# Down products of an expert step run one step later, turned results in two buffers, and a split moved at the second mixer's seam

## The chip, the cores and the metric

The kernel runs on one NeuronCore of one Trainium2 chip. The metric is the device time of one execution in microseconds (us), lower is better. Five engines work beside each other: PE (TensorE, matrix products), DVE (VectorE), ACT (ScalarE), POOL (GpSimd) and SP (SyncE, which here only issues weight loads). They wait for each other through semaphores.

## The reference

A trunk of two residual layers on 256 tokens of width 1024, all float32. Each layer has a mixer (attention and a short gated convolution) and a channel mixer. The channel mixer of the first layer is a dense SwiGLU, that of the second sends each token to 2 of 8 experts:

```python
def swiglu(h, w_gu, w_down):
    gu = h @ w_gu
    g, u = jnp.split(gu, 2, axis=-1)
    return (jax.nn.silu(g) * u) @ w_down

def moe_swiglu(h, router_w, w_gu, w_down):
...
    for e in range(N_EXPERTS):
        out = out + cw[:, e:e + 1] * swiglu(xf, w_gu[e], w_down[e])
```

An expert has 1024 x 7168 gate and up weights and 3584 x 1024 down weights, so that 44 MB are read for each.

## The kernel before, in words

**Halves.** All weights come in pieces of 128 x 2048 floats, 1 MB each, which the kernel calls halves. SP loads a half into one of six slots of `w_raw`. ACT rounds it to a high part (`split_hi`, line 397 or 394), DVE forms the low part as the difference (`split_lo`, line 406 or 403), and PE then multiplies the high and low parts. The parts of a half in the expert section also rotate over six slots (`moe_hi`, `moe_lo`: three of `w_hi`/`w_lo`, then `e_k`/`e_uy`, `hT`/`e_v`, `e_q`/`e_bias`). So the load of half n waits until the low part of half n-6 stands (`lo_ready`), and the split of half n waits until PE has used half n-6 (`half_used`).

**Blocks.** The expert section is eight blocks here, one for each expert, of 42 halves each. Blocks 0, 2, 4 and 6 are wide: 128 tokens, `product` with three products of 512 columns (lines 410 to 412) for each of four pieces, so 12 products to a half. Blocks 1, 3, 5 and 7 are narrow: at most 64 tokens, whose high and low parts lie side by side in one operand, so `both_parts` has two products (lines 1808, 1809) and a half has 8.

**Steps.** A block has seven steps m of 512 hidden columns. A step has four gate and up halves (gate into bank 0, up into bank 1, `up`) and two down halves (`down`, into banks 4 and 5, which gather the whole block). I number the halves of a block 0 to 41 in the order in which PE uses them. Between up and down the hidden values must be turned: in a wide block ACT takes silu of bank 0 (`silu`, line 930), DVE multiplies by bank 1 (`gated`, line 1391), PE transposes into bank 2 (`turn`, line 1814), ACT and DVE make its high and low part (`turn_hi` line 934, `turn_lo` line 1395, tiles `ffT_hi` and `ffT_lo`, which are parts of `cT_hi` and `cT_lo`). In a narrow block ACT copies both banks (`take_gate` line 939, `take_up` line 943), PE turns them and adds the two token halves in one product with the matrix `fold` (`fold_turn`, line 1823), ACT takes silu (`fold_silu`, 947), DVE multiplies (`fold_prod`, 1399), ACT rounds (`fold_hi`, 951), DVE subtracts (`fold_lo`, 1403).

**Order of PE before.** In a step: gate, up, down of the step before, then the turn of this step. A block ends with: down of step 5 (halves 38, 39), turn of step 6, `gather` of the next block's tokens (line 1787, 32 small products, copied to SBUF by `gathered` on ACT line 915/918 and DVE line 1370/1373; its fourth group waits for ACT's first copy), down of step 6 (halves 40, 41). The next block then scales and adds what stands in banks 4 and 5: `take_y` (line 925 on ACT, 1378 on DVE), `scatter` (line 1851) and `add_scattered` (1385).

**Who sets the order.** Every engine's order is written out by hand in its own block; nothing is scheduled. Each engine works strictly in its order.

**Routing.** `route` on DVE ranks the experts; a chain of small POOL instructions then makes the seat tables and ends with `route_ready` (line 708). DVE's first `next_pick` (line 1354) waits for it, in block 0, between the splits of halves 14 and 15. The first `gather` waits for `fold_ready`, the last of `route`'s results (line 1342).

**The second mixer's seam.** Between the dense part and the mixer of layer 2 stands `norm(2)`: DVE adds the sums (line 1121), ACT squares (737), DVE finds the root in a chain of tiny instructions (1096 to 1102) and scales (1109), PE transposes (1580), ACT and DVE split (743, 1126). The second half of that mixer's weights is split by ACT inside the norm and, for its low part, by POOL (`norm_split`).

## Time and profile before

| | us |
|---|---|
| median of 3 runs | 1782.83 (1782.44 to 1782.89) |
| profiled execution | 1784.56 |
| its span, first to last instruction | 1782.7 |
| PE busy | 1669.4 (94%) |
| DVE busy | 1317.7 (74%) |
| ACT busy | 1118.9 (63%) |
| POOL busy | 208.4 (12%) |

The weight loads' queue takes 71.1% of 16 DMA engines' span; 485 MB are read. The expert section runs from about 810 us to 1767 us. Busy shares are averages over stages with different limits, so the rows further below go stage by stage. A row of the timeline gives start, duration, engine, line, tiles and count, and in brackets the idle time of the engine ahead of it and who ended it. The granted clock is given as a share of TensorE's full 2.4 GHz; 0.5 is 1.2 GHz.

### The profile page before, as it was taken

The numbers are of one execution on the slowest core, as the hardware profiler recorded it, in microseconds if no ns is written. First come the engines' busy times: TensorE is split into PE (matmuls) and PEld (weight loads), VectorE is DVE, ScalarE is ACT, GpSimd is POOL, SyncE is SP. The second block draws the span as 40 slices with busy tenths as digits, with TensorE's granted clock in tenths as the row PEclk, the third lists the DMA queues.
The fourth block names the chain that finished last, engine by engine and source line by source line (L and its number), as shares of the span: only waits on it lengthen the run. The fifth ranks groups of instructions, "written<-read, shape, count | busy, mean of one in ns | idle before, by whom it ended". The sixth has DMA issues, their size and how long they took to land.

```text
span 1782.7 us, 22550 instructions
## 1 busy us (share of the span) xinstructions
PE 1669.4 (94%) x7827; PEld 1371.3 (77%) x7827; DVE 1317.7 (74%) x1156; ACT 1118.9 (63%) x1120; POOL 208.4 (12%) x434
## 2 busy tenths in 40 slices
PE   6999999999979999978999989999899999899996
PEld 4888887888768888866787778887778877788784
DVE  4456756544454676566788989889988799898896
ACT  4456643434335567335677877778867688677794
POOL 1034331000010344228200000000000000000000
PEclk8999999999989999977999999999999999999998
DMA  6644554555535445535798999989999989999893
GB/s 267 251 165 166 177 182 151 195 184 190 186 112 180 166 160 177 192 128 207 295 382 331 407 401 348 378 326 397 422 347 365 367 333 423 377 356 376 331 417 144
DMA packets 71783, 488.37 MB, mean 274 GB/s; under 512 B 8667, under 2 KB 11948, under 8 KB 13228
## 3 DMA queue, kind: packets, MB, share of 16 engines
q1 hardware_dynamic: 69052, 483.89, 71.1%
q10 hardware_dynamic: 2672, 3.70, 0.6%
q8 instruction: 36, 0.59, 0.1%
q14 instruction: 23, 0.19, 0.0%
HBM read 484.94 MB, written 2.62 MB: 274 GB/s over the span
## 4 chain that ended last, share of the span: by engine, by line
PE 68%; DVE 14%; issue 7%; DMA 4%; ACT 3%; POOL 3%; DVEq 0%; SPq 0%; ACTq 0%; POOLq 0%
PE bank L410 21%; PE bank L412 20%; PE bank L411 20%; DVE w_lo L406 5%; DMA w_raw<-expert_slabs 4%; DVE e_v L403 3%; DVE e_uy L406 2%; POOL wgtT L699 1%; ACT hT L394 1%; PE bank L1808 1%; DVE e_bias L406 1%; PE bank L1809 1%; PE bank L1649 1%; ACT w_hi L397 1%; PE bank L1814 1%
## 5 line engine op out<-in xcount | busy, mean ns | idle before, releaser
L406 DVE TENSOR_TENSOR w_lo<-w_raw,w_hi 128x2048 fp32r<-128x2048 f32 x285 | 648.8, 2290 | 278.1 <-ACT w_hi L397 277.0
L397 ACT ACTIVATE w_hi<-w_raw 128x2048 fp32r<-128x2048 f32 x289 | 552.0, 1915 | 357.5 <-PE bank L412 351.9
L410 PE MATMUL bank<-w_hi,hT 128*128 128x512 f32 x1072 | 428.1, 399 | 9.7 <-DVE hT L1126 8.9
L412 PE MATMUL bank<-w_hi,hT 128*128 128x512 f32 x1072 | 421.7, 393 | 0.0
L411 PE MATMUL bank<-w_lo,hT 128*128 128x512 f32 x1072 | 421.4, 393 | 0.0
L410 PEld LDWEIGHTS bank<-w_hi,hT 128*128 128x128 f32 x1072 | 204.0, 190 | 54.2 <-DVE hT L1126 10.8
L412 PEld LDWEIGHTS bank<-w_hi,hT 128*128 128x128 f32 x1072 | 203.7, 190 | 43.8
L411 PEld LDWEIGHTS bank<-w_lo,hT 128*128 128x128 f32 x1072 | 204.2, 190 | 41.0
L406 DVE TENSOR_TENSOR e_bias<-w_raw,e_q 128x2048 fp32r<-128x2048 f32 x55 | 125.7, 2286 | 44.5 <-ACT e_q L397 44.5
L397 ACT ACTIVATE e_q<-w_raw 128x2048 fp32r<-128x2048 f32 x55 | 105.6, 1920 | 55.6 <-PE bank L412 36.9
L406 DVE TENSOR_TENSOR e_uy<-w_raw,e_k 128x2048 fp32r<-128x2048 f32 x56 | 129.9, 2320 | 7.4 <-ACT e_k L397 7.1
L403 DVE TENSOR_TENSOR e_v<-w_raw,hT 128x2048 fp32r<-128x2048 f32 x55 | 125.9, 2289 | 10.8 <-ACT hT L394 10.8
L397 ACT ACTIVATE e_k<-w_raw 128x2048 fp32r<-128x2048 f32 x56 | 107.4, 1917 | 30.8 <-PE bank L412 19.7
L1808 PE MATMUL bank<-w_hi,hT 128*128 128x512 f32 x320 | 125.0, 391 | 0.0
L1809 PE MATMUL bank<-w_lo,hT 128*128 128x512 f32 x320 | 124.6, 389 | 0.0
L394 ACT ACTIVATE hT<-w_raw 128x2048 fp32r<-128x2048 f32 x55 | 105.5, 1918 | 24.0 <-PE bank L412 18.0
L1808 PEld LDWEIGHTS bank<-w_hi,hT 128*128 128x128 f32 x320 | 60.1, 188 | 12.7
L1809 PEld LDWEIGHTS bank<-w_lo,hT 128*128 128x128 f32 x320 | 60.1, 188 | 12.5
L410 PE MATMUL bank<-w_hi,cT_hi 128*128 128x512 f32 x168 | 65.9, 392 | 1.5 <-DVE cT_lo L1270 1.5
L412 PE MATMUL bank<-w_hi,cT_lo 128*128 128x512 f32 x168 | 65.5, 390 | 0.0
L411 PE MATMUL bank<-w_lo,cT_hi 128*128 128x512 f32 x168 | 65.4, 389 | 0.0
L1823 PEld LDWEIGHTS bank<-wgt,part 128*128 128x128 f32 x448 | 54.0, 191 | 4.1 <-ACT part L943 1.6
(328 smaller groups left out, 2473.4 us busy)
## 6 DMA issues: line engine op xcount, KB each, us to landing
w_raw<-expert_slabs SPq DMA_DIRECT2D x334, 1024.0 KB, 7.0
w_raw<-mix_slabs SPq DMA_DIRECT2D x88, 1024.0 KB, 4.8
w_raw<-dense_slabs SPq DMA_DIRECT2D x33, 1024.0 KB, 4.8
bias_lines<-bias ACTq DMA_DIRECT2D x2, 768.0 KB, 4.4
X<-in_x SPq DMA_DIRECT2D x2, 512.0 KB, 4.1
bias<-bias_lines SPq DMA_DIRECT2D x1, 1024.0 KB, 7.2
yT<-in_ffn_norm_g ACTq DMA_DIRECT2D x2, 512.0 KB, 5.6
v_buf<-expert_slabs SPq DMA_DIRECT2D x1, 1024.0 KB, 4.8
```

Source lines behind the costliest of these rows:

```text
L394: act.activation(hi_slot(n), in_pair(raw_of(n, early)), ACT.Copy).then_inc(hi_ready, 1)
L397: act.activation(hi_slot(n), raw_of(n, early), ACT.Copy).then_inc(hi_ready, 1)
L403: eng.tensor_tensor(in_pair(lo_slot(n)), in_pair(raw_of(n, early)), hi_slot(n), ALU.subtract).then_inc(lo_ready, 1)
L406: eng.tensor_tensor(lo_slot(n), raw_of(n, early), hi_slot(n), ALU.subtract).then_inc(lo_ready, 1)
L410: pe.matmul(dst, hi, whi, start=first, stop=False, skip_group_check=True)
L411: pe.matmul(dst, hi, wlo, start=False, stop=False, skip_group_check=True)
L412: return pe.matmul(dst, lo, whi, start=False, stop=last, skip_group_check=True)
L699: chain(pool.tensor_tensor(terms[:, :, c, :], src[:, r:r + 2, :], col_no[:, c:c + 1, :].to_broadcast([P, 2, 2 * EXPERTS]), ALU.mult))
L1649: ins = pe.transpose(bank[4 + t][:, P * c:P * c + P], tok_c(rows)[:, t, P * c:P * c + P], ident[:, :])
L1808: pe.matmul(dst, x, whi, start=first, stop=False, skip_group_check=True)
L1809: return pe.matmul(dst, x, wlo, start=False, stop=last, skip_group_check=True)
L1823: ins = pe.matmul(bank[2][:, at:at + NARROW], raw[:, P * j:P * j + P], fold[:, :], start=True, stop=True, skip_group_check=True)
```

## The change

In the expert section the down products of step m-1 move behind gate and up of step m+1: PE's step is now gate(m), turn(m-1), up(m), down(m-2). The block ends with turn(6), gather, down(5), down(6). Since two turned results now live at a time, `ffT_hi`/`ffT_lo` get a second buffer (`zero_r` and a free part of `cT_lo`), picked by the step's parity. SP's loads, ACT's and DVE's lists follow this order; the splits of the next block's halves 42 and 43 (0 and 1 of the next) now stand ahead of the copies of the gathered tokens, that of 44 behind them, and the last two gate/up halves of step 0 in `begin`. New waits: PE's `turn` and `fold_turn` wait for `e_lo` (bank 2 read), each step for `e_silu` (bank 0 read), `silu` and `gated` for a stated `half_used`, `take_gate` for `e_turn`. PE's wait for `fold_ready` moves from ahead of the first gather to behind block 0. At `norm(2)` the split of the mixer's second half stands ahead of the norm on ACT and on DVE; POOL's instruction goes.

```diff
                 def load_step(m, cyc):
                     for i in range(4):
-                        load_half(sp, MOE0 + 4 + i, gate_up(i, m), cyc)
+                        load_half(sp, MOE0 + 8 + i, gate_up(i, m), cyc)
                     for i in range(2):
-                        load_half(sp, MOE0 + 8 + i, down_rows(i, m - 1), cyc)
+                        load_half(sp, MOE0 + 12 + i, down_rows(i, m - 2), cyc)
...
             for layer in range(DEPTH):
-                if layer:
-                    norm_split(2)
-                else:
+                if layer == 0:
                     pool.wait_ge(gsub_ready, 1)
...
             def norm(q):
+                if q == 2:
+                    split_lo(dve, NORM_AT[q] + 1)
                 if q:
                     add_sums(q, 0)
...
             def norm(q):
+                if q == 2:
+                    split_hi(act, NORM_AT[q] + 1)
                 norm_sums(q, 0)
...
                 def narrow_block(b, i2, closing=False):
...
+                    with act.Fori(0, 2) as it:
+                        for j in range(2):
+                            cm = c + 2 * it + j
+                            m = 2 * it + 2 + j
+                            fold_silu(b, m - 1)
+                            take_gate(b, m, MOE0 + 10 + RAW * cm)
+                            split_hi(act, MOE0 + 16, cm)
+                            fold_hi(i2, m - 1, (j + 1) % 2)
+                            take_up(MOE0 + 12 + RAW * cm)
+                            for i in range(17, 22):
+                                split_hi(act, MOE0 + i, cm)
+                    fold_silu(b, MSTEPS - 2)
+                    take_gate(b, MSTEPS - 1, MOE0 + 34 + RAW * c)
+                    split_hi(act, MOE0 + 40, c)
+                    fold_hi(i2, MSTEPS - 2, 1)
+                    take_up(MOE0 + 36 + RAW * c)
+                    split_hi(act, MOE0 + 41, c)
+                    if not closing:
+                        split_hi(act, MOE0 + 42, c)
+                        split_hi(act, MOE0 + 43, c)
+                    fold_silu(b, MSTEPS - 1)
+                    if not closing:
                         gathered(b + 1, 0)
-                    fold_hi(i2, MSTEPS - 1)
+                    fold_hi(i2, MSTEPS - 1, 0)
                     if not closing:
                         gathered(b + 1, 2)
+                        split_hi(act, MOE0 + 44, c)
...
                 def turn(b, m):
                     pe.wait_ge(e_rows, MSTEPS * b + m + 2)
+                    pe.wait_ge(e_lo, MSTEPS * b + m + 1)
...
-                    down(MOE0 + 8, c, b, 0, two, first=True)
-                    turned(b, 1)
-                    with pe.Fori(2, MSTEPS) as m:
-                        cm = c + m - 1
-                        up(MOE0 + 4, cm, 0, two)
-                        up(MOE0 + 6, cm, 1, two)
-                        down(MOE0 + 8, cm, b, m - 1, two)
-                        turned(b, m)
+
+                    def step(n, m, cyc, par, first=False):
+                        pe.wait_ge(e_silu, MSTEPS * b + m)
+                        up(n, cyc, 0, two)
+                        turned(b, m - 1)
+                        up(n + 2, cyc, 1, two)
+                        down(n + 4, cyc, b, m - 2, par, two, first)
+
+                    step(MOE0 + 8, 2, c, 0, first=True)
+                    with pe.Fori(0, 2) as it:
+                        for j in range(2):
+                            step(MOE0 + 14 + 6 * j, 2 * it + 3 + j, c + 2 * it, (j + 1) % 2)
+                    turned(b, MSTEPS - 1)
                     if not closing:
                         pe.wait_ge(spread_ready, 2 * b + 2)
                         if not opening:
                             pe.wait_ge(x_add, 4 * b + 4)
                         gather(b + 1)
-                    down(MOE0 + BLOCK_HALVES - 2, c, b, MSTEPS - 1, two)
-
-                pe.wait_ge(fold_ready, 1)
+                    down(MOE0 + BLOCK_HALVES - 4, c, b, MSTEPS - 2, 1, two)
+                    down(MOE0 + BLOCK_HALVES - 2, c, b, MSTEPS - 1, 0, two)
+
                 gather(0)
                 block(0, opening=True)
...
                 last = pe.value_load(ctl_i[0:1, 0:1], min_val=EXPERTS - 1, max_val=EXPERTS - 1 + SLOTS)
+                pe.wait_ge(fold_ready, 1)
```

What the lists of the engines look like at three places, first before and then after the change (line numbers of the changed kernel are a few higher; ISA, REGISTER_ALU and branch rows only set up what follows).

DVE at the second mixer's seam: the dense part's last rows, then the norm. Before:

```order
L1265 TENSOR_TENSOR rows<-bank,part 128x256
L1276 REGISTER_ALU
L1276 COMPARE_AND_BRANCH
L1270 TENSOR_TENSOR cT_lo<-bank,cT_hi 128x512
L1121 TENSOR_TENSOR X<-X,bank 128x512 x2
L1096 TENSOR_SCALAR nw<-ssq 128x1
```

and after:

```order
L1273 TENSOR_TENSOR rows<-bank,part 128x256
L1284 REGISTER_ALU
L1284 COMPARE_AND_BRANCH
L1278 TENSOR_TENSOR cT_lo<-bank,cT_hi 128x512
L407 TENSOR_TENSOR w_lo<-w_raw,w_hi 128x2048
L1127 TENSOR_TENSOR X<-X,bank 128x512 x2
L1102 TENSOR_SCALAR nw<-ssq 128x1
```

One split, which stood in POOL's list, now stands ahead of DVE's two additions.

PE at the end of a narrow block, from the turn of step 6 (`wgt,part`) over the gather (`aT_hi`, `aT_lo`) to the first down product. Before, with down of step 5 ahead of these rows:

```order
L1823 MATMUL bank<-wgt,part 128x64 x8
L1894 REGISTER_ALU
L1894 COMPARE_AND_BRANCH
L1903 REGISTER_ALU
L1780 ISA
L1787 MATMUL bank<-cT_hi,aT_hi 128x128 x16
L1787 MATMUL bank<-cT_hi,aT_lo 128x128 x8
L1783 REGISTER_ALU
L1787 MATMUL bank<-cT_hi,aT_lo 128x128 x8
L1828 REGISTER_ALU
L1830 REGISTER_ALU
L1808 MATMUL bank<-e_q,cT_hi 128x512
```

and after, with down of step 4 ahead of them:

```order
L1830 REGISTER_ALU
L1831 REGISTER_ALU
L1836 MATMUL bank<-wgt,part 128x64 x8
L1921 REGISTER_ALU
L1791 ISA
L1798 MATMUL bank<-cT_hi,aT_hi 128x128 x16
L1798 MATMUL bank<-cT_hi,aT_lo 128x128 x8
L1794 REGISTER_ALU
L1798 MATMUL bank<-cT_hi,aT_lo 128x128 x8
L1843 REGISTER_ALU
L1819 MATMUL bank<-e_k,zero_r 128x512
```

The first product behind the gather was that of half 40 (`e_q`) with the result turned just before; now it is that of half 38 (`e_k`) with the result of step 5 in the second buffer.

DVE at the same place, from `fold_prod` of step 6 (`rows<-bank,rows`). Before:

```order
L1399 TENSOR_TENSOR rows<-bank,rows 128x256
L1492 REGISTER_ALU
L1492 COMPARE_AND_BRANCH
L1367 REGISTER_ALU
L1373 CAST hT<-bank 128x512
L1402 REGISTER_ALU
L1403 TENSOR_TENSOR cT_hi<-rows,cT_hi 128x4x64
L1367 REGISTER_ALU
L1373 CAST hT<-bank 128x512
L401 ISA
L406 TENSOR_TENSOR e_bias<-w_raw,e_q 128x2048
```

and after:

```order
L407 TENSOR_TENSOR w_lo<-w_raw,w_hi 128x2048
L1407 REGISTER_ALU
L1408 TENSOR_TENSOR rows<-bank,rows 128x256
L1375 REGISTER_ALU
L1381 CAST hT<-bank 128x512
L1411 REGISTER_ALU
L1412 TENSOR_TENSOR cT_hi<-rows,cT_hi 128x4x64
L1375 REGISTER_ALU
L1381 CAST hT<-bank 128x512
L402 REGISTER_ALU
L407 TENSOR_TENSOR e_uy<-w_raw,e_k 128x2048
L402 ISA
```

Behind the two copies of gathered tokens (`hT<-bank`) came the split of half 46, counted on from this block, and four splits of the next block were done; now two are done, and 44 follows.

## Rows read from the trace of the kernel before

**Rows 1.** Page, section 2: GB/s moved in each of 40 slices of the span

```profile
GB/s 267 251 165 166 177 182 151 195 184 190 186 112 180 166 160 177 192 128 207 295 382 331 407 401 348 378 326 397 422 347 365 367 333 423 377 356 376 331 417 144
```

**Rows 2.** Timeline, PE: turns of two successive steps of wide block 0

```profile
890.97 0.60 PE L1814 MATMUL bank<-ident,rows 128*128 128x128 f32 x4
...
907.77 0.60 PE L1814 MATMUL bank<-ident,rows 128*128 128x128 f32 x4
```

**Rows 3.** Stretch of narrow block 1: length, then busy us (instructions) by engine, clock, DMA

```profile
946.50:1058.10 111.60, 101.81 (x502) 83.88 (x502) 104.20 (x72) 91.41 (x76) 0.00 (x0) 0.97 0.95 384
```

**Rows 4.** Timeline, DVE: from one fold_lo to the next in narrow block 1

```profile
1002.04 0.41 DVE L1403 TENSOR_TENSOR cT_hi<-rows,cT_hi 128x256 fp32r<-128x256 f32 x1
1002.37 6.70 DVE L406 TENSOR_TENSOR w_lo<-w_raw,w_hi 128x2048 fp32r<-128x2048 f32 x3
...
1015.93 0.41 DVE L1403 TENSOR_TENSOR cT_hi<-rows,cT_hi 128x256 fp32r<-128x256 f32 x1
```

**Rows 5.** Timeline, ACT: split of half 39 of narrow block 1

```profile
1037.62 1.92 ACT L394 ACTIVATE hT<-w_raw 128x2048 fp32r<-128x2048 f32 x1 [0.57 <-DMA w_raw<-expert_slabs]
```

**Rows 6.** Timeline, four engines: the second mixer's seam

```profile
493.20 1.28 DVE L1121 TENSOR_TENSOR X<-X,bank 128x512 f32<-128x512 f32 x2 [3.17 <-PE bank L412]
...
494.57 1.06 ACT L737 ACTIVATE part<-X 128x1024 f32<-128x1024 f32 x1 [5.26 <-DVE X L1121]
...
497.68 4.50 DVE L1101 TENSOR_TENSOR nw<-nw 128x1 f32<-128x1 f32 x1
...
497.67 4.49 POOL L406 TENSOR_TENSOR w_lo<-w_raw,w_hi 128x2048 fp32r<-128x2048 f32 x1 [191.14 <-ACT w_hi L397]
...
503.74 1.97 PE L1580 MATMUL bank<-ident,q_buf 128*128 128x128 f32 x8 [7.86 <-DVE q_buf L1109]
```

**Rows 7.** Timeline, DVE and PE: block 0 while routing ends

```profile
861.93 0.17 DVE L1354 COPY seat<-seats 128x5 f32<-128x5 f32 x1 [9.53 <-POOL ctl_i L708]
...
863.31 2.28 DVE L403 TENSOR_TENSOR e_v<-w_raw,hT 128x2048 fp32r<-128x2048 f32 x1
...
866.33 0.79 PE L410 MATMUL bank<-e_k,cT_hi 128*128 128x512 f32 x1 [4.18 <-DVE cT_lo L1395]
...
874.18 0.60 PE L1814 MATMUL bank<-ident,rows 128*128 128x128 f32 x4
```

**Rows 8.** Timeline, PE and ACT: ends of wide blocks 0 and 6

```profile
941.37 0.60 PE L1814 MATMUL bank<-ident,rows 128*128 128x128 f32 x4
...
946.46 0.79 PE L410 MATMUL bank<-e_q,cT_hi 128*128 128x512 f32 x1 [0.97 <-DVE cT_lo L1395]
...
953.84 1.27 ACT L925 ACTIVATE cT_hi<-bank,gate 128x512 fp32r<-128x512 f32 x2 [0.92 <-PE bank L412]
...
1653.30 0.60 PE L1814 MATMUL bank<-ident,rows 128*128 128x128 f32 x4
...
1664.32 1.27 ACT L925 ACTIVATE cT_hi<-bank,gate 128x512 fp32r<-128x512 f32 x2 [0.89 <-PE bank L412]
```

**Rows 9.** Timeline, DVE and PE: end of narrow block 1, start of wide block 2

```profile
1039.57 2.29 DVE L403 TENSOR_TENSOR e_v<-w_raw,hT 128x2048 fp32r<-128x2048 f32 x1 [0.20 <-ACT hT L394]
...
1055.23 1.76 PE L1787 MATMUL bank<-cT_hi,aT_lo 128*128 128x128 f32 x8 [2.02 <-ACT hT L918]
1058.14 0.79 PE L1808 MATMUL bank<-e_q,cT_hi 128*128 128x512 f32 x1 [1.14 <-DVE cT_hi L1403]
1075.71 0.49 PE L410 MATMUL bank<-e_q,hT 128*128 128x512 f32 x1 [0.84 <-ACT part L930]
```

**Rows 10.** Stretch at the same seam (columns as in Rows 3)

```profile
1055.40:1062.30 6.90, 5.76 (x18) 4.70 (x19) 3.21 (x5) 1.25 (x3) 0.00 (x0) 0.51 1.02 423
```

**Rows 11.** Page, section 5: weight loads of all 28 narrow turns, 16 each

```profile
L1823 PEld LDWEIGHTS bank<-wgt,part 128*128 128x128 f32 x448 | 54.0, 191 | 4.1 <-ACT part L943 1.6
```

**Rows 12.** Timeline, DVE and ACT: end of the last narrow block

```profile
1750.02 2.29 DVE L403 TENSOR_TENSOR e_v<-w_raw,hT 128x2048 fp32r<-128x2048 f32 x1 [0.21 <-ACT hT L394]
...
1766.90 1.26 ACT L925 ACTIVATE cT_hi<-bank,gate 128x512 fp32r<-128x512 f32 x2 [4.62 <-PE bank L1809]
```

304 lines of the change are left out of this document (150 added, 154 removed).

## The prediction, made before the changed kernel ran

> **What bounds the kernel now.** I read the page first, then the busy times of stretches, then the timelines of each kind of seam. The expert section is more than half of the span, and its two kinds of block have two different bounds.
>
> A wide step takes 16.80 us from turn to turn [rows 2]. Its 72 products and four transposes follow each other without a gap: with 0.36 us for the transposes and 0.13 us to get going, a half takes 2.72 us and 24 products 5.44 us. PE is the bound. A narrow step takes 13.89 us [rows 4]: six low parts at about 2.2 us and two fold operations at 0.33 us of pitch leave DVE without idle time. DVE is the bound there, 104.2 us busy of 111.6 in block 1 [rows 3], and PE, with 8 products or 1.82 us for a half and 1.7 us for a fold turn (54.0 us over 28 turns is 1.9, less the tail that overlaps the next product) [rows 11], would need 12.6. In the last two steps of a narrow block ACT waits for the load itself [rows 5]; at about 420 GB/s [rows 1] a half of 1.049 MB takes 2.5 us.
>
> So a step in mid-block has nothing to give: where PE is the bound it doesn't wait, and where it waits it isn't the bound. What can be won lies at the seams.
>
> **Steady steps: 0.** Both kinds keep their instructions, bytes and slots. In a wide step the new wait for `e_rows` at turn(m-1) is fed by a multiplication that can start after up(m-1); at least 10 us of down and gate products hide it. In a narrow step `take_up` now follows `fold_hi` of the step before, which follows DVE's split of the half that PE needs just ahead of that turn; copy and PE's half end together, about 1.4 and 1.8 us after that split. Behind that wait in PE's list stands up(m), but it has to wait for DVE's next split anyway. If the cover were gone, each of some 24 narrow steps would pay what is missing.
>
> **The second mixer's seam: 3.9 us less.** DVE's tiny L1101 takes 4.50 us instead of 0.16, together with POOL's split of 4.49 [rows 6]. POOL's goes, so 4.34 come back. DVE's own split (2.3 us) lies where DVE idles 3.17 us, and ACT's where ACT idles 5.26 [rows 6]: ACT is free at 489.3, rounds until 491.2, DVE subtracts until 493.7, 0.5 us after it was wanted at 493.2. 4.34 - 0.5 = 3.9. PE's idle 7.86 us shrinks to about 4; if the low clock behind it stays until the same time, 2 us are left; if it ends early, 6.
>
> The same row meets a rule of the Trainium skill, SBUF — State Buffer, section "Who interferes with whom": DVE with two SBUF inputs and GpSimd exclude each other for a whole instruction. By that rule the stall is POOL's doing and goes with it; were it chance, the term would be -0.5. The trace agrees with the rule, 4.50 beside 4.49.
>
> **The opening of block 0: 3.7 us less.** The first gather no longer waits for the fold matrix, and starts 5 to 6 us sooner; but the end of routing, at 861.93 on DVE [rows 7], hangs on POOL's chain and stays. DVE is held there, between the splits of 14 and 15, before as after; half 15 is ready at 863.31 + 2.2 = 865.5. Before, PE also wanted the turned result of step 1 for halves 14 and 15, started them at 866.33 after 4.18 idle and reached the next turn at 874.18: 7.85 us for 5.44 us of products, so 2.4 went to the low clock. Now halves 14 and 15 are gate(3): 14 is done before the stall, only 15 is left at 865.5. PE idles longer, about 7 us, so I charge the low clock again: 15 takes some 5 us, to 870.5. 874.2 - 870.5 = 3.7; without the low clock it waits for `gated` until 869.0, and 5.2 are won; with a longer one 2.
>
> **Wide to narrow, four seams: 7.6 us less.** Before, from the last turn (941.37) PE gathers, waits 0.97 us for the turned low part, and multiplies halves 40 and 41 [rows 8]. Now it gathers and multiplies 38 to 41, while ACT and DVE make the parts. For DVE, the bound of what follows, the time counts from "half 37 used" to ACT's `take_y`. Before: halves 38 and 39 (5.44) and 941.37 to 953.84 (12.47), 17.9. Now turn and gather 4.1, four halves 10.9, 0.3 to start: 15.3. That wins 2.6. The last such seam, without the low clock, had 1653.30 to 1664.32, 11.02: 16.5, so 1.15. Of the four seams two are of either kind: 2 x 2.6 + 2 x 1.15 = 7.6 (5 to 9). From `take_y` on, DVE has the same list and the loads stand as far ahead.
>
> **Narrow to wide, three seams: 13.2 us less.** Count from the end of DVE's split of half 39, 1039.57 + 2.2 = 1041.8 [rows 9]. Before, PE needs down(5), turn(6), the gather with 2.02 us idle for ACT's copy, 1.14 us idle for `fold_lo`, down(6) at a clock of 0.51 [rows 10], the next block's first four halves, and after 0.84 us for silu it starts the fifth at 1075.7: 33.9 us; the three seams lie within 0.8 us. Now: `fold_prod`, `fold_hi`, `take_up`, at 1.4; turn(6) to 3.1; three gather groups to 5.9. ACT's first copy now stands behind the splits of 41, 42 and 43 and `fold_silu`. The landings pace these at 2.5 us each, so it ends at about 8.2. The fourth group ends at 9.1, down(5) at 12.8, down(6) at 16.4, four wide halves at 27.3. PE is the bound from here, so 6.6 us are won, 6.4 over the three, with no low clock. But PE runs right behind DVE at the end of a narrow block and now sits idle before turn(6): half 37 is used 1.8 us after its split, turn(6) may start 6.3 us after it, 4.4 us idle. Before this idle was 1.5. Like the 4.18 us of rows 7 it should bring the low clock; part of it lies beside the wait for the copy. I charge 2.0 (0 to 3.5): 4.4 x 3 = 13.2 (9 to 19).
>
> **The last block: 2.0 us less.** From split 39 (1752.2) to `take_y` (1766.90) 14.7 us [rows 12]. Now turn(6) at 3.1, then down(5), down(6): 11.0 with 0.3 to start 11.2, 3.5 less; 1.5 for the low clock.
>
> **Sum.** 3.9 + 3.7 + 7.6 + 13.2 + 2.0 = 30.4. The profiled execution took 1784.56 with a span of 1782.70; it would come to 1754.2, the span to 1752.3. The median of 1782.83 lies 1.7 below that execution, so 1752.4 for the new median.
>
> **Rivals.**
> *The clock eats the seams.* The long idle before turn(6) brings a low clock that lasts over gather and down(5), down(6). 3.5 to 4 us more of such products at half speed than I charge would leave 1 us at each of the three seams, 0 in the last block, 2.5 in block 0, 2.5 at the mixer's: 2.5 + 2.5 + 7.6 + 3 = 15.6, 1767. For: 0.51 in rows 10 after smaller gaps.
> *No low clock at all.* 3.9 + 5.2 + 7.6 + 19.2 + 3.5 = 39.4, 1743.4. For: two wide-to-narrow seams had 1 us of idle and none.
> *Loads take it back.* What DVE wins at the start of a narrow block it waits for at its end, since loads were already late there: 30.4 - 7.6 = 22.8, 1760. Against: the load's lead is rebuilt in each wide block, where a half takes 2.72 us and a load 2.5.
> *Slower.* In narrow steps PE no longer has the down products as a backlog; it waits for each half from DVE, 0.4 us six times. If these gaps bring the low clock often, PE becomes the bound: 12.6 us of work take 12.6/(1 - f/2) when a share f of the time is at 0.5. That passes 13.9 at f = 0.19, and the 30 us are gone, over 24 steps, at 15.2 us a step, f = 0.34. At f = 0.45 a step takes 16.3: 24 x 2.4 - 30 = +27, 1810. Against: gaps of 0.9 us once a step left the clock of block 1 at 0.97 [rows 3], and a slow stretch closes the gaps that caused it.
> A page bears on this rival: the Trainium skill, TensorE: Matmul & The Clock Gate, section "HAM oscillation — how this bites in real kernels", tells of a kernel whose products wait for every slice of weights and begin each at the low clock. No row here shows that for gaps as short as 0.4 us.
> *It doesn't do what it says.* The turn, not the halves, stays late (`take_up` behind a late `fold_prod`), and what is won at the seam is lost in steps: within 3.5 us of before.
>
> **How the numbers follow.** Forecast as summed, with its own range of 1746 to 1761: 0.52. Loads take it back, 1760: 0.06. Clock eats the seams, 1761 to 1770: 0.20. No low clock, 1740 to 1746: 0.13. Slower, 1786.5 and up: 0.05. No change: 0.04. The range 1740 to 1768 holds a little over 8 in 10 and takes in the bounds of the terms (2 + 2 + 5 + 9 + 0.5 = 18.5 to 6 + 5.2 + 9 + 19 + 3.5 = 42.7). A measurement of this kernel can tell 0.2%, 3.6 us, from no change: faster 0.91, same 0.04, slower 0.05.
>
> **What would show it.** Wide steps still 16.80 and narrow ones 13.9. DVE's L1101 (a few lines lower after the change) at 0.16 us everywhere in the second mixer's norm. The first product after the stall near 865.5 less 3.9. No idle time of PE between gather and down at any seam; from DVE's split of half 39 to the fifth half of the wide block 29 to 30 us. An idle of about 4 us before the last turn of a narrow block. Wrong would be: narrow steps above 14.5, a mean clock below 0.95, or a PE wait for `e_lo` or `e_rows` inside a step.

## The result

The changed kernel takes 1772.01 us (median of 4 runs, 1770.75 to 1775.7) where the kernel before, beside it, takes 1782.86 (1782.44 to 1783.16). The ratio is 0.9934, with a 95% interval of 0.9914 to 0.9954: 10.8 us less. The sign was forecast, the size was not: 30.4 us were summed, and 1772 lies above the stated range of 1740 to 1768.

The profiled execution has a span of 1774.0 us and took 1775.7, against a span of 1782.7 before, so 8.7 us are to be explained in the trace. That execution is the slowest of its four, 3.7 us above their median. ACT's `take_y` divides the expert section into blocks. Its starts give this account (us; in the narrow rows T39 is the end of DVE's split of half 39, its start plus 2.2 us, as in the forecast). The forecast's 13.2 for the narrow-to-wide seams was counted up to the wide block's fifth half; by its working (down(6) ends at 16.4, 0.3 to start, 2.0 for the clock) 18.7 us was to be T39 to `take_y`, and the rest, 2.5 over the three, falls in the wide blocks:

| stretch | before | after | change | forecast |
|---|---|---|---|---|
| start to the first wide-to-narrow `take_y` | 953.84 | 940.93 | -12.9 | -10.2 |
| three wide blocks, `take_y` to `take_y` | 126.07, 127.63, 126.08 | 124.21, 124.06, 124.27 | -7.2 | -7.5 |
| four narrow blocks, `take_y` to T39 | 87.94, 88.10, 87.84, 87.90 | 90.64, 89.00, 89.74, 89.92 | +7.5 | 0 |
| three narrow-to-wide seams, T39 to `take_y` | 22.33, 21.92, 22.57 | 23.49, 22.94, 22.39 | +2.0 | -10.7 |
| last block, T39 to `take_y` | 14.68 | 16.62 | +1.9 | -2.0 |
| last `take_y` to the end | 15.8 | 15.8 | 0 | 0 |
| sum | | | -8.7 | -30.4 |

What stands above the narrow rows came, with 2.4 us to spare. The narrow blocks were to give 12.7 and cost 11.4.

Of the first row 1.5 us are no effect of the change: the last transposes of the dense part, ahead of everything that was changed, start at 488.1 in the trace before and at 486.6 after, and between 486.8 and 489.5 in the twelve traces of the experiments. So a difference of 2 or 3 us between the spans of two traces says little.

### The profile page after: what moved, and what is told of

Its sections match the earlier page's. It is cut to its first block, busy times and chain, and to the rows that moved or that the text cites. A ratio compares the mean times of both kernels' runs of the same rounds, so it can differ in the third digit from the quotient of the medians.

```text
span 1774.0 us, 22510 instructions
## 1 busy us (share of the span) xinstructions
PE 1681.5 (95%) x7827; PEld 1390.1 (78%) x7827; DVE 1312.4 (74%) x1157; ACT 1118.5 (63%) x1120; POOL 202.9 (11%) x433
## 4 chain that ended last, share of the span: by engine, by line
PE 47%; DVE 8%; issue 7%; ACT 4%; POOL 3%; DMA 2%; DVEq 0%; ACTq 0%; SPq 0%; POOLq 0%
PE bank L411 13%; PE bank L413 12%; PE bank L412 12%; DVE w_lo L407 3%; DMA w_raw<-expert_slabs 2%; PE bank L1798 2%; DVE e_v L404 2%; PE bank L1819 2%; PE bank L1820 2%; ACT w_hi L398 2%; PE bank L1836 1%; DVE e_uy L407 1%; POOL wgtT L697 1%; PE bank L1826 1%; ACT hT L395 1%
## 5 line engine op out<-in xcount | busy, mean ns | idle before, releaser
L411 PE MATMUL bank<-w_hi,hT 128*128 128x512 f32 x912 | 365.0, 400 | 9.7 <-DVE hT L1132 8.9
L413 PE MATMUL bank<-w_hi,hT 128*128 128x512 f32 x912 | 359.0, 394 | 0.0
L412 PE MATMUL bank<-w_lo,hT 128*128 128x512 f32 x912 | 358.4, 393 | 0.0
L411 PEld LDWEIGHTS bank<-w_hi,hT 128*128 128x128 f32 x912 | 173.7, 190 | 47.9 <-DVE hT L1132 10.8
L413 PEld LDWEIGHTS bank<-w_hi,hT 128*128 128x128 f32 x912 | 173.2, 190 | 37.4
L412 PEld LDWEIGHTS bank<-w_lo,hT 128*128 128x128 f32 x912 | 174.0, 191 | 34.7
L404 DVE TENSOR_TENSOR e_v<-w_raw,hT 128x2048 fp32r<-128x2048 f32 x55 | 125.8, 2287 | 16.4 <-ACT hT L395 16.1
L413 PE MATMUL bank<-w_hi,cT_lo 128*128 128x512 f32 x328 | 128.2, 391 | 0.0
L398 ACT ACTIVATE e_q<-w_raw 128x2048 fp32r<-128x2048 f32 x55 | 105.6, 1920 | 14.9 <-PE bank L413 10.2
L411 PE MATMUL bank<-w_hi,cT_hi 128*128 128x512 f32 x264 | 103.2, 391 | 1.5 <-DVE cT_lo L1278 1.5
L412 PE MATMUL bank<-w_lo,cT_hi 128*128 128x512 f32 x264 | 102.7, 389 | 0.0
L1836 PE MATMUL bank<-wgt,part 128*128 128x64 f32 x448 | 60.2, 293 | 22.5 <-DVE zero_r L1412 20.9
L1836 PEld LDWEIGHTS bank<-wgt,part 128*128 128x128 f32 x448 | 60.3, 211 | 26.9 <-issue 25.2
L413 PEld LDWEIGHTS bank<-w_hi,cT_lo 128*128 128x128 f32 x328 | 61.6, 188 | 13.5
L1819 PE MATMUL bank<-w_hi,hT 128*128 128x512 f32 x160 | 62.5, 391 | 0.1
```

Of the source, the lines that this page charges most:

```text
L398: act.activation(hi_slot(n), raw_of(n, early), ACT.Copy).then_inc(hi_ready, 1)
L404: eng.tensor_tensor(in_pair(lo_slot(n)), in_pair(raw_of(n, early)), hi_slot(n), ALU.subtract).then_inc(lo_ready, 1)
L411: pe.matmul(dst, hi, whi, start=first, stop=False, skip_group_check=True)
L412: pe.matmul(dst, hi, wlo, start=False, stop=False, skip_group_check=True)
L413: return pe.matmul(dst, lo, whi, start=False, stop=last, skip_group_check=True)
L1819: pe.matmul(dst, x, whi, start=first, stop=False, skip_group_check=True)
```

## The profile after, beside the rows of before

**The second mixer's seam** [rows 6]. Timeline of the changed kernel, DVE and PE (start, duration, engine, line, operation, tiles, count; in brackets the idle time ahead and what ended it):

```profile
489.64 2.29 DVE L407 TENSOR_TENSOR w_lo<-w_raw,w_hi 128x2048 fp32r<-128x2048 f32 x1 [1.11 <-ACT w_hi L398]
...
494.39 0.15 DVE L1102 TENSOR_SCALAR nw<-ssq 128x1 f32<-128x1 f32 x1 [1.27 <-ACT part L735]
...
494.95 0.16 DVE L1106 TENSOR_TENSOR nw<-nwi 128x1 f32<-128x1 f32 x1
495.15 0.16 DVE L1107 TENSOR_TENSOR nw<-nw 128x1 f32<-128x1 f32 x1
```

```profile
498.04 1.97 PE L1591 MATMUL bank<-ident,q_buf 128*128 128x128 f32 x8 [3.67 <-DVE q_buf L1115]
```

No instruction of the tiny chain is longer than 0.16 us, L1107 (the old L1101, 4.50 us in rows 6) among them, and POOL has no instruction in this window. From the end of the dense products to the first transpose it was 13.56 us, with 7.86 of idle; now it is 9.37 with 3.67.

**The opening of block 0** [rows 7]. Timeline of the changed kernel, DVE and PE:

```profile
855.40 0.17 DVE L1362 COPY seat<-seats 128x5 f32<-128x5 f32 x1 [16.13 <-POOL ctl_i L706]
```

```profile
859.12 0.79 PE L411 MATMUL bank<-hT 128*128 128x512 f32 x1 [7.48 <-DVE e_v L404]
```

DVE stands 16.13 us for POOL's chain. PE is idle for 7.48 us ahead of half 15, the second of gate(3), and starts it at half clock (0.79 and 0.63 us where 0.49 and 0.39 are usual): the forecast's "about 7 us" and its charge.

**A narrow step** [rows 4]. Timeline of the changed kernel, DVE and then ACT, around a fold:

```profile
987.42 0.42 DVE L1408 TENSOR_TENSOR rows<-bank,rows 128x256 f32<-128x256 f32 x1
987.76 2.28 DVE L407 TENSOR_TENSOR e_bias<-w_raw,e_q 128x2048 fp32r<-128x2048 f32 x1
989.96 0.42 DVE L1412 TENSOR_TENSOR cT_hi<-rows,cT_hi 128x256 fp32r<-128x256 f32 x1
990.62 6.70 DVE L407 TENSOR_TENSOR w_lo<-w_raw,w_hi 128x2048 fp32r<-128x2048 f32 x3 [0.24 <-ACT w_hi L398]
```

```profile
987.88 0.42 ACT L956 ACTIVATE cT_hi<-rows 128x256 fp32r<-128x256 f32 x1 [0.79 <-DVE rows L1408]
988.20 0.58 ACT L948 ACTIVATE part<-bank 128x512 f32<-128x512 f32 x1
988.68 3.71 ACT L398 ACTIVATE w_hi<-w_raw 128x2048 fp32r<-128x2048 f32 x2
```

DVE is no longer without idle time: 0.24 us behind `fold_lo` (L1412), for ACT's rounding. ACT's `fold_hi` (L956) can start only when DVE has done `fold_prod` (L1408); `take_up` (L948) now follows it, and only then the split. The 0.42, 0.58 and 1.9 us, with their overlaps, end near 990.6, and DVE has been ready since 990.4. Before, the split followed `fold_hi` at once. The step is 14.20 us instead of 13.89.

The first step of a narrow block lost time in another way. PE waits there for DVE's `add_scattered` ahead of a scatter (L1865), and soon after that the clock falls. One row of PE, and the busy times of the stretch (us, then busy time and count of PE, weight loads, DVE, ACT and POOL, the granted clock, the DMA share and GB/s):

```profile
960.52 0.50 PE L1865 MATMUL bank<-cT_hi 128*128 128x512 f32 x1 [2.01 <-DVE X L1393]
```

```profile
961.40:964.90 3.50, 3.50 (x13) 2.92 (x12) 3.50 (x4) 1.21 (x1) 0.00 (x0) 0.51 1.02 428
```

All four narrow blocks of the changed kernel have such a stretch (3.4, 3.4, 3.4 and 6.8 us), and none of the kernel before has. The idle time ahead is 2.01, 1.56, 1.93 and 2.01 us, where it was 1.48 to 1.55, so its length alone doesn't tell when the clock falls.

**Narrow to wide** [rows 9, 10]. Timeline of the changed kernel at the end of block 1, DVE, then PE:

```profile
1029.36 2.29 DVE L404 TENSOR_TENSOR e_v<-w_raw,hT 128x2048 fp32r<-128x2048 f32 x1 [0.19 <-ACT hT L395]
1031.57 0.42 DVE L1408 TENSOR_TENSOR rows<-bank,rows 128x256 f32<-128x256 f32 x1
1031.91 2.29 DVE L407 TENSOR_TENSOR e_bias<-w_raw,e_q 128x2048 fp32r<-128x2048 f32 x1
1034.12 0.42 DVE L1412 TENSOR_TENSOR zero_r<-rows,zero_r 128x256 fp32r<-128x256 f32 x1
1034.75 6.83 DVE L407 TENSOR_TENSOR w_lo<-w_raw,w_hi 128x2048 fp32r<-128x2048 f32 x3 [0.21 <-ACT w_hi L398]
```

```profile
1034.68 3.65 PE L1836 MATMUL bank<-wgt,part 128*128 128x64 f32 x16 [5.58 <-DVE zero_r L1412]
1038.09 3.65 PE L1798 MATMUL bank<-cT_hi,aT_hi 128*128 128x128 f32 x16
1041.54 3.62 PE L1798 MATMUL bank<-cT_hi,aT_lo 128*128 128x128 f32 x16
1044.96 0.73 PE L1819 MATMUL bank<-e_k,zero_r 128*128 128x512 f32 x1
```

and the busy times of stretches (columns as above):

```profile
1024.00:1033.00 9.00, 5.10 (x23) 3.90 (x21) 8.56 (x6) 7.72 (x9) 0.00 (x0) 1.00 1.01 421
1033.00:1050.00 17.00, 15.32 (x60) 14.28 (x61) 10.28 (x9) 8.71 (x8) 0.00 (x0) 0.50 0.96 399
1268.60:1285.70 17.10, 14.34 (x58) 13.50 (x59) 11.35 (x10) 8.60 (x10) 0.00 (x0) 0.50 1.01 420
1507.60:1521.30 13.70, 13.18 (x55) 12.62 (x56) 9.12 (x9) 6.26 (x7) 0.00 (x0) 0.50 1.01 422
1743.10:1753.30 10.20, 8.60 (x28) 7.55 (x29) 4.60 (x5) 2.44 (x3) 0.00 (x0) 0.50 0.01 2
```

T39 is 1031.6. The last turn starts 3.1 us behind it, not 1.4, because it waits for `fold_lo` (L1412), and between `fold_prod` and `fold_lo` DVE splits half 40. PE is idle for 5.58 us, and then the clock is at its lower level, 0.50, for 17 us: turn (3.65 us, 1.89 before), gather (3.65 and 3.62, 1.98 and 1.95 before) and down(5) all run in it. Before, 6.9 us stood at 0.51 [rows 10]. The other two seams have 4.88 and 5.46 us of idle and then 17 and 14 us at 0.50. The last block, where the down products stand right behind the turn, has 10 behind 4.97 us of idle. From T39 to the fifth half of the wide block (1065.65) it is 34.1 us, where the forecast had 29 to 30 and the kernel before 33.9. In the page the changed kernel's turns show it too:

```profile
L1836 PE MATMUL bank<-wgt,part 128*128 128x64 f32 x448 | 60.2, 293 | 22.5 <-DVE zero_r L1412 20.9
```

## The experiments

Each kernel ran in rounds beside the kernel before. That took 1786.93 us in the first four experiments (1783.87 to 1788.62), 1788.0 in the next four (1782.96 to 1788.77), and 1785.84 in the last four (1782.58 to 1789.68), a few us more than in the first comparison, so ratios are to be compared, not times. The changed kernel itself was not run again beside them, so a difference between an experiment and it rests on two comparisons, and one of under 3 us says nothing. Part of the spread of the kernel before can be seen: seam_fold_only and before_gather_fill have the last narrow block unchanged, and T39 to `take_y` takes 17.98 and 17.88 us there, against 14.68 in the trace before. In these two the clock fell twice in that stretch, for 3.4 us each, behind idle times of 1.9 to 2.1 us; in the trace before it didn't.

| kernel | median us | ratio to before [95%] |
|---|---|---|
| changed kernel | 1772.01 | 0.9934 [0.9914, 0.9954] |
| seam_fold_only | 1780.45 | 0.9963 [0.9949, 0.9977] |
| down_before_gather | 1766.16 | 0.9882 [0.9862, 0.9901] |
| fill_idle | 1752.67 | 0.9823 [0.9795, 0.9851] |
| take_up_late | 1771.32 | 0.9921 [0.9904, 0.9939] |
| folds_earlier | 1758.18 | 0.9835 [0.9816, 0.9853] |
| earlier_and_late | 1757.16 | 0.9829 [0.9810, 0.9848] |
| fill_and_late | 1757.21 | 0.9831 [0.9812, 0.9851] |
| earlier_late_and_swap | 1754.9 | 0.9832 [0.9815, 0.9848] |
| early_late_gather_fill | 1751.78 | 0.9812 [0.9796, 0.9828] |
| before_gather_fill | 1784.92 | 0.9991 [0.9979, 1.0004] |
| half_bytes_after | 1770.81 | one run |
| half_bytes_before | 1776.2 | one run |

The phases of the narrow blocks in their profiled executions (us):

| kernel | narrow blocks, `take_y` to `take_y` | of it T39 to `take_y` |
|---|---|---|
| before | 110.27, 110.02, 110.41, 102.58 | 22.33, 21.92, 22.57, 14.68 |
| changed kernel | 114.13, 111.94, 112.13, 106.54 | 23.49, 22.94, 22.39, 16.62 |
| down_before_gather | 110.43, 110.04, 111.90, 107.15 | 21.00, 20.25, 20.87, 16.56 |
| fill_idle | 106.29, 105.48, 106.58, 100.18 | 17.15, 16.87, 17.08, 12.65 |
| take_up_late | 111.96, 111.86, 112.53, 103.44 | 23.48, 23.08, 22.20, 16.17 |
| folds_earlier | 109.18, 110.76, 109.42, 100.60 | 19.59, 19.95, 18.83, 9.89 |
| earlier_and_late | 108.78, 108.86, 108.39, 99.41 | 19.76, 18.90, 18.57, 11.53 |
| fill_and_late | 108.66, 107.67, 108.00, 102.49 | 18.96, 18.71, 18.67, 12.65 |
| earlier_late_and_swap | 105.78, 107.88, 107.41, 101.18 | 16.59, 18.24, 17.11, 11.54 |
| early_late_gather_fill | 105.91, 105.73, 105.66, 100.53 | 16.73, 16.92, 16.75, 11.54 |
| before_gather_fill | 109.67, 110.05, 112.45, 105.57 | 22.02, 22.04, 24.30, 17.88 |

In the four kernels with earlier folds the split of half 39 stands behind the folds of step 5, so their T39 is compared only among themselves and with their expectations.

### seam_fold_only: the small part of the change

On the kernel before:

```diff
-                if layer:
-                    norm_split(2)
-                else:
+                if layer == 0:
...
+                if q == 2:
+                    split_hi(act, NORM_AT[q] + 1)
...
+                if q == 2:
+                    split_lo(dve, NORM_AT[q] + 1)
...
-                pe.wait_ge(fold_ready, 1)
                 gather(0)
...
+                pe.wait_ge(fold_ready, 1)
```

> The kernel before with only the two small parts of the change: the split at the second mixer's seam, and the later wait for the fold matrix. The traces of before and after put 4.2 us on the seam (13.56 us from the dense part's last down product to the norm's first transpose before, 9.37 after). Theory A (the fold wait alone gives nothing, since routing ends when it ends): 4 to 5 us less than before, 1778. Theory B (the earlier gather also lets routing on POOL end sooner, as it did by about 1 us in the changed kernel): 5 to 6.5 us less, 1777.

Measured: 0.9963, 6.6 us less. The first wide-to-narrow `take_y` stands at 948.84, 5.0 sooner than before. 0.8 of it stand ahead of the mixer, 4.2 are the seam, so the wait for the fold matrix by itself gave nothing: routing, counted from the mixer's first transposes, ended 0.6 us sooner, and the low clock behind it lasted 10 us where it lasted 7. That is theory A. The blocks behind are as before, but for the last one, which lost 3 us in the profiled execution to the low clock told of above (its last step took 10.86 us instead of 9.19). So about half of the change's gain, 0.0037 of 0.0066, needs none of the new order of PE's list. That order brought 0.9934 against 0.9963, some 5 us, but the two intervals overlap.

### down_before_gather: the same idle time, other products behind it

On the changed kernel, narrow and wide blocks alike:

```diff
+                        down(MOE0 + BLOCK_HALVES - 4, c, b, MSTEPS - 2, 1, two)
                         gather(b + 1)
-                    down(MOE0 + BLOCK_HALVES - 4, c, b, MSTEPS - 2, 1, two)
+                    else:
+                        down(MOE0 + BLOCK_HALVES - 4, c, b, MSTEPS - 2, 1, two)
```

> The changed kernel, but at the end of each block down(5) stands ahead of the gather: turn(6), down(5), gather, down(6). The idle of 5.6 us ahead of turn(6) stays. Theory A (the low clock at the narrow-to-wide seam lasts 17 us because only small products, turn and gather, follow the idle; large ones end it sooner): the low stretch shrinks to 7 to 10 us, split 39 to take_y from 23 us to 19 to 20, 3 us less at each of three seams, about 1762. Theory B (the length of the idle alone sets it): the low stretch stays 17 us, the time within 2 us of the changed kernel's 1772.

Measured: 0.9882, by the ratios 9 us below the changed kernel, by the medians as they stand 6, by the profiled spans 6.6. Timeline of PE, and the same stretch as above:

```profile
1035.87 3.65 PE L1836 MATMUL bank<-wgt,part 128*128 128x64 f32 x16 [4.91 <-DVE zero_r L1412]
1039.27 0.77 PE L1819 MATMUL bank<-e_k,zero_r 128*128 128x512 f32 x1
...
1045.02 1.90 PE L1798 MATMUL bank<-cT_hi,aT_hi 128*128 128x128 f32 x16
1046.75 1.95 PE L1798 MATMUL bank<-cT_hi,aT_lo 128*128 128x128 f32 x16
```

```profile
1033.00:1050.00 17.00, 14.13 (x71) 12.74 (x72) 11.56 (x10) 9.91 (x11) 0.00 (x0) 0.70 1.01 419
```

The idle time ahead of the turn is about what it was, 4.91 us (5.58, 4.88 and 5.46 at the three seams of the changed kernel), and the turn runs at half clock as before. But now down(5), which is products of 512 columns without a gap, follows, and the gather behind it runs at full clock: 1.90 and 1.95 us. The mean clock of the stretch is 0.70 where it was 0.50, and the low stretches at the three seams last 10, 7 and 10 us instead of 17, 17 and 14. With the gather first, the clock stayed low through turn, gather and down. T39 to `take_y` is 2.5, 2.7 and 1.5 us shorter at the seams, 6.7 in all. The same idle time in the same place costs less when other products stand behind it: theory A, though with 2.2 us a seam and not 3. The wide blocks are 1.2 to 1.3 us shorter too. No low clock stood there, so this has another cause, which no run isolates.

### fill_idle: the idle time filled

On the changed kernel, products that nobody reads, into a bank that is free there:

```diff
+                    if two:
+                        pe.wait_ge(x_add, 4 * b + 4)
+                        for _ in range(FILL):    # FILL = 20
+                            pe.matmul(bank[3][:, :], hr_hi[:, 0, 0:P], hr_hi[:, 0, 0:CHUNK], start=True, stop=True,
+                                      skip_group_check=True)
                     turned(b, MSTEPS - 1)
```

> The changed kernel, with 20 products of 512 columns into a free bank ahead of turn(6) in narrow blocks; nothing reads their result. They take 4.5 us at full clock of the 5.6 us in which PE idles. Theory A (the idle brings the low clock, and that costs 6 to 7 us a seam): granted clock 1.0 through turn and gather, split 39 to take_y 16 to 17.5 us instead of 23 at three seams, and about 12 instead of 16.6 in the last block: 20 us or more less than the changed kernel, about 1750. Theory B (clock is not what costs; ACT's and DVE's hand-overs do): within 3 us of 1772.

Measured: 0.9823, some 20 us below the changed kernel. Timeline of PE, and the stretch:

```profile
1028.48 4.70 PE L1921 MATMUL bank<-aT_hi 128*128 128x512 f32 x20
1033.54 1.97 PE L1837 MATMUL bank<-wgt,part 128*128 128x64 f32 x16 [0.37 <-DVE zero_r L1413]
1035.32 1.98 PE L1799 MATMUL bank<-cT_hi,aT_hi 128*128 128x128 f32 x16
1037.14 1.06 PE L1799 MATMUL bank<-cT_hi,aT_lo 128*128 128x128 f32 x8
1038.92 1.11 PE L1799 MATMUL bank<-cT_hi,aT_lo 128*128 128x128 f32 x8 [0.73 <-ACT hT L922]
```

```profile
1033.00:1050.00 17.00, 15.90 (x93) 13.82 (x93) 15.12 (x12) 13.99 (x13) 0.00 (x0) 1.00 1.01 419
```

The turn starts at T39 + 3.1 us, as late as in the changed kernel, and waits for the same `fold_lo`. What differs is the clock: 1.00 in place of 0.50, turn 1.97 us in place of 3.65, each part of the gather 1.98 in place of 3.65. T39 to `take_y` falls from 23.5, 22.9, 22.4 and 16.6 to 17.1, 16.9, 17.1 and 12.6. So at a seam the low clock cost 6.3, 6.1 and 5.3 us, and 4.0 in the last block, where the forecast charged 2.0 and 1.5, and the late turn by itself cost less than half a us (17.1 against the 16.4 + 0.3 of the forecast's working without its charge).

### take_up_late: the hand-off in a narrow step

On the changed kernel, ACT splits one half more before it copies bank 1:

```diff
                             fold_hi(i2, m - 1, (j + 1) % 2)
+                            split_hi(act, MOE0 + 17, cm)
                             take_up(MOE0 + 12 + RAW * cm)
-                            for i in range(17, 22):
+                            for i in range(18, 22):
```

> The changed kernel with one pair swapped in ACT's list of a narrow step: the split of the next half stands ahead of take_up instead of behind it. Theory A (DVE's 0.24 us of idle in each narrow step comes from ACT's fold_hi, take_up and split in a row behind fold_prod): steps of 14.20 go to 13.89; loads then bound the last steps at 14.9, so 1 us or less is won in each narrow block, 2 to 4 in all, 1769. Theory B (loads are the bound already at 14.2 us a step): steps stay, no change.

Measured: 0.9921, 2 us below the changed kernel by the ratios, with intervals that overlap. The steps are 13.88 us, so the three operations in a row were the cause of 14.20:

```profile
990.79 0.42 DVE L1413 TENSOR_TENSOR cT_hi<-rows,cT_hi 128x256 fp32r<-128x256 f32 x1
991.12 2.28 DVE L407 TENSOR_TENSOR w_lo<-w_raw,w_hi 128x2048 fp32r<-128x2048 f32 x1
```

But the faster steps meet the loads. The steps end in 14.9 us ones earlier, and `take_y` to T39 is 88.48, 88.78, 90.33, 87.27, in all 4.4 us less than in the changed kernel. The edit touches four steps of a block, which at 0.32 us are 5.1 over the four blocks, and two of the blocks (the first and the last) escaped the low clock of their first step, 0.5 and 1.6 us more. So some 3 us were lost again. ACT's waits for loads in blocks 3 to 7 (us in total, times, longest), in the changed kernel and in this one:

```profile
ACT hT L395 <- DMA w_raw<-expert_slabs: 2.0, 4, 0.6
...
ACT w_hi L398 <- DMA w_raw<-expert_slabs: 0.9, 2, 0.6
ACT e_k L398 <- DMA w_raw<-expert_slabs: 0.9, 2, 0.6
```

```profile
ACT hT L395 <- DMA w_raw<-expert_slabs: 5.2, 10, 0.6
...
ACT e_k L398 <- DMA w_raw<-expert_slabs: 4.0, 7, 0.6
...
ACT w_hi L398 <- DMA w_raw<-expert_slabs: 3.7, 7, 0.6
```

3.8 us have become 12.9; with block 1, 9.9 have become 16.5.

### half_bytes_after and half_bytes_before: what the loads cost

The edit is the same in both, and leaves half of each expert half's weights unread, so that the sums of the experts are not the reference's:

```diff
+            if n >= MOE0:
+                sp.dma_start(w_raw[:, n % RAW, 0:HALF // 2], src[:, 0:HALF // 2]).then_inc(landed[n % RAW], 16)
+            else:
                 sp.dma_start(w_raw[:, n % RAW, :], src).then_inc(landed[n % RAW], 16)
```

> The changed kernel, with each load of a half of the expert section moving only the first half of its bytes; the products read what the buffer held before in the other half, so the sums of the experts are not the reference's, while every instruction of the engines stays. If the steps of 14.9 us near the end of a narrow block are due to the loads: every step of every narrow block is 14.20 us, ACT has no wait for a load there, T39 comes 1.5 to 2.5 us sooner after take_y, and the profiled time falls by 6 to 10 us. If they are due to something on the engines, steps of 14.9 stay. Wide blocks, which PE bounds, keep 16.80 us a step.

> The kernel before, with each load of a half of the expert section moving only the first half of its bytes; the other half of the weights is what the buffer held, so the sums of the experts are not the reference's, while every instruction of the engines stays. It is the partner of half_bytes_after. All narrow steps should be 13.89 us. take_y to T39 is 87.9 us in the kernel before; if the loads cost it as much as the changed kernel (0.3 to 2 us a block) it is 86 to 87.6, if less, the change itself brought the loads onto the path, and it stays at 87.8 or more.

Measured: with half the bytes every full narrow step is 14.20 or 14.21 us after the change (one of 14.67 in the last block apart) and 13.89 or 13.90 before it, and no wait of ACT for a load is left. `take_y` to T39 is 88.61, 88.98, 89.17 and 88.15 after, 87.35, 87.35, 87.36 and 85.98 before. Each is one execution. Against the full loads that is 2.0, 0.0, 0.6 and 1.8 us of load cost after the change, 4.4 in all, and 0.6, 0.7, 0.5 and 1.9 before it, 3.7 in all. The changed kernel paid the loads only 0.7 us more than before. The seams don't move: T39 to `take_y` 23.42, 22.96, 22.61 with half the bytes. Their cost has nothing to do with the loads. The span of the changed kernel fell by 4.9 us, less than the 6 to 10 expected.

The two runs also show what the changed kernel loses without the loads: 1.3, 1.6, 1.8 and 2.2 us a block. Four full steps at 0.32 are 1.3. The rest, 0.4, 0.5 and 0.9, is in the blocks where the first step had the low clock behind the scatter's wait; the first block had none, and no rest.

### folds_earlier and earlier_and_late: no filler, another order

In the last step of a narrow block the folds of step 5 stand two halves earlier, on ACT and on DVE (DVE's part shown, the loop peeled so that halves 38 and 39 follow the folds):

```diff
                     fold_prod(b, i2, MSTEPS - 2)
-                    split_lo(dve, MOE0 + 40, c)
+                    split_lo(dve, MOE0 + 38, c)
                     fold_lo(b, MSTEPS - 2, 1)
-                    split_lo(dve, MOE0 + 41, c)
+                    for i in range(39, 42):
+                        split_lo(dve, MOE0 + i, c)
```

earlier_and_late is this and take_up_late together.

> The changed kernel, with the folds of step 5 two halves earlier in the last step of a narrow block: fold_prod(5) ahead of DVE's split of half 38, fold_lo(5) behind it, ACT's fold_hi and take_up beside them, and then the splits of 39, 40 and 41. No filler, the same instructions in number and kind. Theory A (the seam costs what it does because turn(6) waits for the turned low part of step 5 behind two more splits, and the idle time then brings the low clock): turn(6) can start about 0.5 us after the products of half 37, PE idles ahead of it for 1 to 2 us instead of 5.6, the granted clock stays high at the narrow-to-wide seams or falls for under 7 us, and T39 to take_y comes to 17 to 19 us (22.9 in the changed kernel), counted from DVE's split of half 39, which itself moves 0.4 us back. Total 1751 to 1759 us. Theory B (what counts is any idle time of PE at the seam, wherever it lies): the idle moves to the wait for halves 38 and 39, the low clock comes all the same, and the total is 1764 to 1772 us.

> folds_earlier, and besides ACT splits half 17 (and its like) ahead of take_up, as in take_up_late. If ACT's three operations in a row are what DVE waits for behind fold_lo, the steps of narrow blocks are 13.88 us instead of 14.20 until the loads bind, and the total is 0 to 2 us below folds_earlier, since the loads took back nearly all of it in take_up_late. If the loads take back only what the seam then hides, both add up: 2 to 4 us below folds_earlier.

Measured: 0.9835 and 0.9829, by the ratios 18 and 19 us below the changed kernel (14 and 15 by the medians as they stand), nearly what the filler brought, with no work added. T39 to `take_y` is 18.6 to 20.0 us at the seams, at and just above the 17 to 19 expected. Neither theory was quite right on the way there. Timeline of PE in earlier_and_late:

```profile
1029.04 1.97 PE L1856 MATMUL bank<-wgt,part 128*128 128x64 f32 x16 [0.45 <-DVE zero_r L1424]
1030.81 1.98 PE L1818 MATMUL bank<-cT_hi,aT_hi 128*128 128x128 f32 x16
1032.63 1.06 PE L1818 MATMUL bank<-cT_hi,aT_lo 128*128 128x128 f32 x8
1039.39 1.97 PE L1818 MATMUL bank<-cT_hi,aT_lo 128*128 128x128 f32 x8 [5.70 <-ACT hT L921]
```

The idle ahead of the turn is 0.45 us, so turn and three quarters of the gather run at full clock. But 5.70 us of idle now stand behind them, ahead of the fourth group, for ACT's first copy (L921), which is behind the splits of halves 39 to 43 in ACT's list. The low clock sets in within that idle time (at 1035.7) and lasts 10 us; at the other two seams it lasts 7. Theory B had the idle moving (to another place, though), theory A the total.

### earlier_late_and_swap and early_late_gather_fill: the idle time that is left

The first is earlier_and_late with the edit of down_before_gather. The second is earlier_and_late with 20 unread products into bank 0 inside `gather`, ahead of its fourth group:

```diff
                         if i == 3:
+                            for _ in range(fill):    # 20 ahead of a wide block, else 0
+                                pe.matmul(bank[0][:, :], hr_hi[:, 0, 0:P], hr_hi[:, 0, 0:CHUNK], start=True, stop=True,
+                                          skip_group_check=True)
                             pe.wait_ge(xg_act, 2 * g + 1)
```

> earlier_and_late, and besides down(5) stands ahead of the gather at the end of a narrow block. In earlier_and_late PE idles 0.45 us ahead of turn(6), and 5.70 us ahead of the gather's fourth group, for ACT's copy of the first group, which stands behind ACT's splits. Theory C (the seam's cost is one idle time of some 6 us that the order of PE's list only moves, and with it comes the low clock): down(5), 3.7 us of products, fills the stretch ahead of the gather, so 2 to 3 us of idle are left, the low clock lasts under 7 us, T39 to take_y falls by 2 to 3 us, and the total is 6 to 10 us below earlier_and_late. Rival D (the gather then starts 3.7 us later, its copies and the next block's first half with it, and DVE and ACT lose what PE wins): the total stays within 3 us of earlier_and_late.

> earlier_and_late, with 20 unread products of 512 columns into bank 0 ahead of the gather's fourth group where the next block is wide, where PE idles 5.70 us. If the low clock is what is left of the seam's cost: no stretch of low clock at the narrow-to-wide seams, T39 to take_y 2 to 4 us shorter, total 8 to 12 us below earlier_and_late, about 1746 us, and below fill_idle. If the seam is bound by ACT and the loads: T39 to take_y shorter by under 1 us and the total within 3 us.

Measured: 0.9832 for the swap, no different from earlier_and_late: rival D had the total. The seams were 3.2, 0.7 and 1.5 us shorter in the trace, the last block 1.8 longer, so D's reason is not shown. Its idle time ahead of the fourth group was 1.96 us, with 0.94 more behind it, and a low clock of 7 us came all the same. The filler took the low clock away at all three seams and T39 to `take_y` fell by 3.0, 2.0 and 1.8 us, as expected. But the total came to 0.9812, by the ratios 3 us below earlier_and_late and not 8 to 12; the profiled spans differ by 8.3, and the intervals leave room for both. Busy times of its first seam and of a narrow block show what comes next:

```profile
1028.00:1045.00 17.00, 15.52 (x92) 13.42 (x92) 14.71 (x11) 12.95 (x11) 0.00 (x0) 1.00 1.01 420
1171.60:1277.40 105.80, 101.67 (x516) 84.76 (x517) 102.65 (x70) 91.57 (x77) 0.00 (x0) 1.00 1.00 402
```

The clock of the seam is 1.00. But the DMA engines are busy for all of the block's 105.8 us, at 402 GB/s, against 0.94 and 380 GB/s in block 1 of the changed kernel and a narrow block of 110 to 114 us. A block needs 42 halves of 1.049 MB, 44.0 MB; 105.8 us at that rate bring 42.5. By this estimate the block lives on a lead of 1.5 halves that the wide block built up, and at 105.7 us a narrow block is at the limit of its loads. fill_idle, whose steps still take 14.21 us, comes to the same 105.48 in one block. No run thinned the loads of a repaired kernel, so the limit is argued and not shown.

### fill_and_late

> fill_idle (20 unread products of 512 columns ahead of the last turn of each narrow block) together with take_up_late. The seams should stay at the high clock as in fill_idle (T39 to take_y 17.1 us), the narrow steps 13.88 until the loads bind. If the loads take back the gain of the steps: within 1.5 us of fill_idle, 1751 to 1754 us on a chip where that takes 1752.7. If not: 4 to 6 us less.

Measured: 0.9831 beside fill_idle's 0.9823, within the 1.5 us of the first case. Steps are 13.88 us at first and 14.91 at the end, and `take_y` to T39 comes to 89.71, 88.97, 89.35 and 89.85, not less than fill_idle's 89.14, 88.61, 89.50 and 87.53: ACT waits for loads for 16.5 us there in all, against 9.1.

But the seams did not stay as in fill_idle. T39 to `take_y` is 1.6 to 1.8 us longer at all three, since a low clock of 3.4 us came back. Timeline of PE at the first:

```profile
1034.08 1.97 PE L1838 MATMUL bank<-wgt,part 128*128 128x64 f32 x16 [0.89 <-DVE zero_r L1414]
1039.70 1.28 PE L1800 MATMUL bank<-cT_hi,aT_lo 128*128 128x128 f32 x8 [0.96 <-ACT hT L922]
1040.77 0.74 PE L1821 MATMUL bank<-e_k,zero_r 128*128 128x512 f32 x1
```

Here two idle times of under 1 us, with only the turn and three groups of the gather between them, were enough. Their length alone doesn't decide it: at the third seam they were 0.88 and 0.66 us and the clock fell, while fill_idle had 0.94 and 0.65 there and stayed at 1.00.

### before_gather_fill: was it the clock alone?

On the kernel before, 9 unread products ahead of the gather's fourth group, where PE idled for 2.02 us [rows 9]:

> The kernel before, with 9 unread products of 512 columns into bank 0 ahead of the gather's fourth group where the next block is wide; there PE idled 2.02 us, and a low clock began some 3 us later and lasted 6.8 us at each of three seams. If PE's idle time brings that low clock too: down(6) and the next block's first halves run at the high clock, T39 to take_y is 2 to 3.5 us shorter at the three seams, and the total 6 to 10 us below the kernel before, 1773 to 1777 us on a chip where that takes 1783. If the low clock has another cause (the turns and gathers themselves, whose products are short): within 2 us of before.

Measured: 0.9991, no difference. The clock behaved as expected in part (the low stretch is 3.4 us at two of the seams instead of 6.8), but 1.80 us of idle still stand ahead of down(6), for `fold_lo`, and T39 to `take_y` is 22.02 and 22.04 us, as before. (The third, 24.30, had a wait of 2.1 us for a load in its last step.) So the filler is no gift by itself: the change plus a PE that is kept busy gives some 31 us, while the change alone gives 11 and the 9 products alone nothing clear of noise. What the kernel before would take with no low clock at all at its seams was not measured.

## Why the prediction was wrong, and where it was right

**The second mixer's seam: right.** Forecast 3.9, measured 4.2, with the DVE row gone to 0.16 us and PE's idle at 3.67. The page SBUF — State Buffer of the Trainium skill, section "Who interferes with whom", made the stall POOL's doing; the trace agrees, the stall went with POOL's instruction.

**The opening and the first wide to narrow seam: right.** 3.7 and 2.6 forecast. From the end of routing to the next turn it was 12.25 us and is 8.12, so 4.1; from there to `take_y` 79.66 and 77.41, so 2.3. Routing, which was to stay, ended 0.8 us sooner, counted from the mixer's first transposes. Some 1.5 us more stand ahead of the mixer, by chance.

**Wide to narrow: right.** The three wide blocks gave 1.9, 3.6 and 1.8, 7.2 in all against 7.5. The block with 3.6 is the one that had the low clock at its end before, as the forecast's two kinds of seam have it. (2 x 2.6 + 2 x 1.15 is 7.5, where the forecast wrote 7.6.)

**Narrow to wide: the step that failed.** The sum had "turn(6) to 3.1" and "I charge 2.0 (0 to 3.5)". Two things were wrong. The first is a wait that was missed: in the new order `fold_turn` waits for `e_lo`, and `fold_lo` of step 5 stands behind a whole split of 2.2 us. PE's idle was put at 4.4 and was 5.6. By itself this cost some 0.4 us a seam (fill_idle). The second is the size of the charge: the low clock behind that idle cost 5.3 to 6.3 us a seam, about three times the charge and one and a half to nearly two times the upper bound. The charge came from a row in which PE came back with products of 512 columns [rows 7]; here it came back with turn and gather, and the clock stayed at 0.50 until down(5) was under way or through. The trace before had a row of the other kind, which the forecast didn't use, the first gather of the expert section:

```profile
810.10 3.64 PE L1787 MATMUL bank<-cT_hi,aT_hi 128*128 128x128 f32 x16 [6.70 <-DVE wgt L1342]
```

It took 3.64 us for 16 products that take 1.98 at full clock, and the first products of 512 columns behind it still ran at 0.63 us each, for 5 us. The rival "the clock eats the seams" had the mechanism, and at 1767 was still too mild: it left 1 us of gain at each seam, where 0.7 was lost. It deserved more than 0.20: the working itself had said that the idle would grow from 1.5 to 4.4.

**The last block: the same step.** 1.5 charged, 4.0 measured, and the turn at T39 + 3.1 again. (Its 11.0 us behind T39 doesn't follow from the forecast's own terms, 3.1 for the turn and 3.7 and 3.6 for the down products, which give 10.4.)

**Steady steps at 0: the second failure.** "Copy and PE's half end together" looked at PE and `take_up`, and not at what follows `take_up` on ACT: DVE, which bounds the step, waits for that split behind `fold_lo`. With the loads thinned, `take_y` to T39 differs by 6.9 over the four blocks (354.9 and 348.0), and 0.7 of loads make the 7.5 that were measured. 0.32 us over four full steps of four blocks are 5.1 of it; take_up_late, which takes them away, shows the cause. The other 1.8 came with the low clock of the first step, which the forecast did not have either.

**Loads take it back: not the cause, but the limit.** The changed kernel pays the loads 0.7 us more than the kernel before. They do cap what a repair can bring: take_up_late lost some 3 us again while ACT's waits for loads grew by 6.6, and with seam and step both repaired the narrow blocks stand at 105.7 us with the DMA engines busy throughout.

**No low clock at all.** This rival said 1743.4, 39.4 less. With the clock out of the seams, fill_idle is 31.6 us below before by the ratio, and 35.5 by the spans of the profiled executions (1747.2 and 1782.7). Two terms are short of the forecast: `take_y` to T39 is 3.0 us longer over the four blocks, in place of 0, and T39 to `take_y` won 17.8 (5.2, 5.1, 5.5, 2.0) in place of 20.2.

**Slower by many short idle times: it did not come as told.** In the stretch from 1024 to 1033 us of the changed kernel, the last of its narrow steps, PE was busy for 5.10 of 9.00 us at a granted clock of 1.00. But it was not only the long idle times that brought the low clock: 1.6 to 2.0 us did in the first step of each narrow block, for 3.4 to 6.8 us, and 0.89 and 0.96 us in fill_and_late.

What stays open: why the clock stays low through the turn and the gather and rises within down products. The runs show which products stood behind the idle time in each case, and nothing of what the chip counts. Open, too, is why idle times of about 2 us in the first narrow step brought the low clock in some blocks and not in others (in two of four in take_up_late). Also open are single late loads: one for which ACT waits 2.10 us, with a step of 16.4, in before_gather_fill, and one of 2.12 us in earlier_late_and_swap, of which I saw the wait and not its reason.

## What to carry to other kernels

When a change makes PE wait less often but longer in one place, the cost of that place is not the idle time but the idle time and all products that follow at half clock; take the length of that stretch from what PE will run next, and put the order so that a long run of products of 512 columns stands behind it. An operation that is moved past another on an engine that is not the bound still counts if the bounding engine waits for what is now behind it: follow the hand-off one operation further than the moved one. And before a seam is repaired, work out the time in which the loads of that stretch can come at all, since no repair there can win more.

## What the runs showed of the hardware

- After 4.9 to 5.6 us of PE idle the granted clock was 0.50 for 14 to 17 us when products of 64 and 128 columns (turn and gather) came first, and, after 4.9 to 5.1 us of idle, for 7 to 10 when the turn was followed by products of 512 columns. The Trainium skill, TensorE: Matmul & The Clock Gate, section "HAM oscillation — how this bites in real kernels", tells of idle time between bursts that brings the low clock; the trace agrees, with 0.50 behind each of these idle times.
- 20 unread products of 512 columns, 4.70 us of PE time in each narrow block, made the kernel 20 us faster (fill_idle against the changed kernel, by the ratios).
- A low clock of 3.4 us also followed an idle time of 2.01 us (first step of a narrow block), and of 0.88 and 0.66 us with short products between them (fill_and_late); behind 0.94 and 0.65 us in the same place the clock stayed at 1.00 (fill_idle).
- With 5.70 us of idle cut to 1.08 by such products, the clock of the seam stayed at 1.00; with 1.96 and 0.94 us of idle and short products between them it still fell for 7 us.
- Half the bytes in each load took 8.4 us off the span of the kernel before (1782.7 to 1774.3) and 4.9 off that of the changed one (1774.0 to 1769.1), though the weight loads fill only 71% of the DMA engines' time.
